# Swapping sample and prompt in the order of units of a hybrid trunk step

## The reference

```python
def trunk_layer(x, mod, p, ssd_h0, gdn_h0, kv_ctx):
    h = rmsnorm(x, p['norm1_w']) * (1.0 + sc1) + sh1
    u = h @ p['w_in']                       # 2584 columns, four head groups
    y = concatenate([ssd(u), gated_deltanet(u), fnet(u), attention(u)]) @ p['w_out']
    x = x + g1 * y                          # g1, sc1, sh1 ...: from silu(c) @ w_mod + b_mod
    h2 = rmsnorm(x, p['norm2_w']) * (1.0 + sc2) + sh2
    return x + g2 * peer(h2, p['peer_w_q'], p['peer_keys'], p['peer_u'], p['peer_v'])

def peer(x, w_q, sub_keys, u_tab, v_tab):   # 8 heads x 16 of 16384 experts a token
    idx, gate = ...                         # two-level top 16 of q @ keys
    act = gelu(einsum('ted,td->te', u_tab[idx], x))
    return einsum('te,ted->td', gate * act, v_tab[idx])
```

## Time and profile before

| | us |
|---|---|
| median of three runs | 3529.52 |
| lowest and highest | 3523.68, 3545.67 |
| the profiled execution | 3547.55 |
| its span in the profile | 3545.7 |

### The profile page before, as it was taken

How to read it: one execution, slowest core, us unless ns; L and a number is a source line. 1 busy time by engine, 2 the same in 40 slices (tenths; PEclk the granted TensorE clock), 3 DMA queues, 4 the chain that set the end, 5 groups by cost and what they waited for, 6 DMA issues and landing times.

```text
span 3545.7 us, 28928 instructions
## 1 busy us (share of the span) xinstructions
PE 2157.3 (61%) x10824; PEld 1423.2 (40%) x10824; DVE 1777.1 (50%) x3941; ACT 349.2 (10%) x765; POOL 1705.3 (48%) x1540
## 2 busy tenths in 40 slices
PE   7799446665893455537877766665885100027787
PEld 6689445553550355533525235553561000001111
DVE  0331477885119777791410457886107888850000
ACT  0211111111210000011111011111110000000000
POOL 0000045344334678874554556444334577776664
PEclk6775778786897555568998988786897555569999
DMA  5424268446685899998889888445676699999998
GB/s 158 154 72 137 81 237 325 143 161 218 222 300 213 316 395 394 395 381 298 310 324 334 316 292 324 166 161 195 225 273 216 218 367 369 371 372 369 346 367 314
DMA packets 380348, 960.02 MB, mean 271 GB/s; under 512 B 40857, under 2 KB 181529, under 8 KB 380081
## 3 DMA queue, kind: packets, MB, share of 16 engines
q0 software_dynamic: 221184, 805.40, 61.9%
q1 hardware_dynamic: 155456, 150.41, 12.9%
q10 hardware_dynamic: 3568, 2.36, 0.2%
HBM read 955.70 MB, written 2.36 MB: 270 GB/s over the span
## 4 chain that ended last, share of the span: by engine, by line
PE 22%; POOL 20%; DVE 17%; DMA 16%; issue 10%; ACT 2%; another core or an unknown queue 1%; POOLq 0%; SPq 0%; DVEq 0%; ACTq 0%
POOL sb_ring L550 20%; PE pb L571 15%; DMA sb_ring<-in_peer_v,sb_idxT 6%; PE pv L571 5%; DMA sb_wring<-in_w_in 4%; DVE sb_ring L1830 4%; DMA sb_wring<-in_peer_w_q 2%; DMA sb_ring<-in_peer_u,sb_idxu 2%; PE pb L574 1%; DVE sb_i16u L1759 1%; DMA sb_wring<-in_w_out 1%; DVE sb_pos L1759 1%; DVE sb_xe L1754 1%; ACT sb_hT L1050 1%; DVE sb_big L1536 1%
## 5 line engine op out<-in xcount | busy, mean ns | idle before, releaser
L550 POOL DMA_INDIRECT sb_ring<-in_peer_u,sb_idxu x768 | 963.4, 1254 | 1053.2 <-DVE sb_gatew L1802 461.7
L550 POOL DMA_INDIRECT sb_ring<-in_peer_v,sb_idxT x768 | 741.8, 966 | 766.3 <-PE pv L571 524.7
L1830 DVE CUSTOM_DVE_ANT_0 sb_ring<-sb_ring,sb_h 128x1024 f32<-128x1024 f32 x768 | 923.5, 1224 | 175.1 <-DMA sb_ring<-in_peer_u,sb_idxu 150.1
L571 PE MATMUL pv<-sb_ring,sb_wcol 128*32 128x512 f32 x3072 | 712.9, 652 | 163.1 <-DMA sb_ring<-in_peer_v,sb_idxT 136.5
L571 PE MATMUL pb<-sb_hT,sb_wring 128*128 128x256 f32 (+1 forms) x2304 | 439.7, 355 | 152.7 <-ACT sb_hT L1050 59.1
L571 PEld LDWEIGHTS pb<-sb_hT,sb_wring 128*128 128x128 f32 x2304 | 383.9, 212 | 226.6 <-ACT sb_hT L1050 61.5
L571 PEld LDWEIGHTS pv<-sb_ring,sb_wcol 128*32 128x32 f32 x3072 | 131.3, 115 | 687.1 <-DMA sb_ring<-in_peer_v,sb_idxT 454.9
L571 PE MATMUL pb<-sb_big 128*128 128x128 f32 (+2 forms) x1888 | 256.4, 307 | 64.9 <-DVE sb_big L1536 40.1
L571 PEld LDWEIGHTS pb<-sb_big 128*128 128x128 f32 (+1 forms) x1888 | 248.9, 217 | 81.7 <-DVE sb_big L1536 46.8
L571 PE MATMUL pb<-sb_cT,sb_wring 128*128 128x2 f32 x768 | 167.7, 353 | 144.8 <-DMA sb_wring<-in_w_mod 144.8
L574 PE MATMUL pb<-sb_cst,sb_dots 128*128 128x128 f32 x6 | 2.9, 475 | 391.1 <-DMA sb_ring<-in_peer_v,sb_idxT 364.3
(11 more groups left out here) (218 smaller groups left out, 1729.9 us busy)
## 6 DMA issues: line engine op xcount, KB each, us to landing
sb_wring<-in_w_mod SPq DMA_DIRECT2D x48, 1024.0 KB
sb_wring<-in_w_in SPq DMA_DIRECT2D x40, 1024.0 KB
sb_wring<-in_peer_w_q SPq DMA_DIRECT2D x32, 1024.0 KB
sb_wring<-in_w_out SPq DMA_DIRECT2D x16, 1024.0 KB
sb_ring<-in_peer_u,sb_idxu POOLq DMA_INDIRECT x768
sb_ring<-in_peer_v,sb_idxT POOLq DMA_INDIRECT x768
sb_cst<-in_cst SPq DMA_DIRECT2D x1, 1544.0 KB, 6.3
out<-sb_h ACTq DMA_DIRECT2D x3, 512.0 KB, 2.6
```

Of the source, the lines that this page charges most:

```text
L550: pool.indirect_dma_start(ring[:, j, :], None, a["tab_" + kind][l_of(q)], bass.IndirectOffsetOnAxis(ap=of, axis=0)).then_inc(rows_in[j], 16)
L571: return nc.tensor.matmul(out, lhsT, rhs, start=start, stop=stop)
L1830: dve.tensor_tensor_reduce(out=ring[:, j, :], in0=ring[:, j, :], in1=h2[:, t, :], scale=1.0, scalar=0.0, op0=ALU.mult, op1=ALU.add, accum_ ...
```

## The change

The list of units is turned within each layer: the sample comes first, then the prompt. With it the running numbers of tiles change, so that slots 0 to 3 begin at 0, 2, 3 and 5.

```diff
 GROUP_TILES = [[0], [1, 2]]
-UNITS = [(0, 0), (1, 0), (0, 1), (1, 1)]
+UNITS = [(1, 0), (0, 0), (1, 1), (0, 1)]
...
 def seq_tiles(u):
 
-    first = [0, 1, 3, 4][u]
+    first = [0, 2, 3, 5][u]
     return [(first + i, t) for i, t in enumerate(GROUP_TILES[UNITS[u][0]])]
```

## The result

| | before | after |
|---|---|---|
| median, us | 3532.5 (four runs) | 3692.1 (four runs) |
| lowest and highest | 3523.7, 3545.7 | 3681.9, 3708.0 |
| profiled execution (span) | 3547.55 (3545.7) | 3681.86 (3680.1) |

The ratio is 1.045, with a 95% interval of 1.040 to 1.050: the turned order is 4.5% slower, where 3725 us (5.5%) had been forecast. The same change timed on a second chip gave 1.050 [1.043, 1.058]. The two profiled executions lie at opposite ends of their ranges, so their spans differ by 134 us where the medians differ by 160.

The account below looks back on a forecast made before the run. The kernel was taken as paced by DMA where it is busy and by the mix's chain elsewhere. Slots 0 to 3 and tail: 244 + 170 + 7 + 145 - 370 = +196 us, on the median 3529.5 + 196 = 3725 us; range 3630 to 3850.

Parts of the forecast that it names:

- The blocks: Slot 0: the 16 blocks of w_mod sums woven into it cost 4.7 us each, 75 us in all.
- The sample's mix alone: Slot 0: 700 us of slot 3 less 66, 31 and 97, plus 31 us of block waits: 537 us.
- The dots half: Slots 1 and 3, up to the end of the intra stage: 256 rows with their dots and ten w_in blocks, 416 us.
- DVE becomes the bound: Slots 1 and 3, intra stage: dots and mix on DVE outlast the rows by 23 us, plus 12 in short stages.
- the tail's 177 us: Time of 128 rows in the tail, taken as the pace for 256 rows in slots 1 and 3: 354 us.
- The v half: Slots 1 and 3, after the dots: 188 + 186 us, twelve weight blocks, one handover and a hole, 446 us.
- The hole of 20 us: Slots 1 and 3, query stage: the next tile's v items must wait for its end; 80 matmuls without v, about 20 us.
- the handover: Slots 1 and 3: one change from dots to v matmuls, about 20 us.
- the one for fewer batches: Slot 2's mix: 17 of 64 batches lie in the sums, so 17/64 of 97 us of dots and v matmuls go, 26 us.
- Rival 1: Slots 1 and 3 run at 387 GB/s, 753 us each; kernel 3491 us on the median, 1.1% faster; chance 4%.
- Rival 2: Slots 1 and 3: the mix adds to the gathers, 950 us each, 160 us more together, 3885 us; chance 10%.
- rival 3: Slot 0's 16 blocks hide (-75 us) and layer 1's sums run at 2.4 GHz (-54): 3596 us, 1.9% slower; chance 12%.

Follow-up runs that it names:

- the freed `gelu`: The changed kernel with `gelu` and `end` also allowed at the points inside the query stage: 3604.7 us, 1.032 of the kernel before.

## Why the prediction was right, and where it wasn't

**The account by slot held.** Lost cover of the sample's mix, two slots of a fixed length under a prompt, one tile saved at the end; predicted and measured span by slot: 707 and 704, 870 and 846, 907 and 887, 870 and 851, 388 and 392. In sum 3742 and 3680 us, 62 us too much.

**Slot 0.** Right in sum through two errors of opposite sign. The blocks cost 58 us and not 75. The sample's mix alone had been put at 537 us, from slot 3's chain less the shares of dots, v matmuls and block waits; from its first normalisation (96 us) to the slot's end (704) it is 608 us, less 58, so 550. Taking shares of a chain away left 13 us too little. That the sum came within 3 us is luck.

**Slots 1 and 3.** The size was nearly right, the reason wrong. The dots half was forecast at 416 us and took 418. But it was built from 354 us of rows at the tail's pace, 27 us for bytes of the weight blocks, and 35 us in which "DVE becomes the bound". The bytes have no part in it (rows of half the length don't shorten it), and it isn't DVE that is late: POOL is. The step that failed is the reading of the tail's 177 us as the pace of transfers. The same row has POOL busy for 136.21 us with 129 gathers, and with 0.30 us between two of them that is 136 + 39 = 175 of the 177. POOL was the limit there, at 1.07 us a gather, and under denser dots a gather takes 1.34 (331.55 us for 248). 248 x (1.34 + 0.30) = 406 of the 418 us. So the match of 416 and 418 is luck. The sign stood in the trace of the kernel before, whose chain over the whole span has POOL's gathers first:

```profile
by line: POOL sb_ring L550 19.9%; PE pb L571 15.4%; issue 9.7%; DMA sb_ring<-in_peer_v,sb_idxT 6.4%; PE pv L571 4.9%; DMA sb_wring<-in_w_in 4.5%; DVE sb_ring L1830 4.1%; DMA sb_wring<-in_peer_w_q 2.1%; DMA sb_ring<-in_peer_u,sb_idxu 2.0%; P
```

The v half was forecast at 446 us, with 8 more for the unit's end, and took 428. The hole of 20 us was there (19 and 19 by the freed `gelu`). What was mis-sized are the terms beside the tail's 188 + 186 us and the hole: 32 us for the bytes of twelve weight blocks, 20 for the handover and 8 for the end, 60 us, which measured 428 - 374 - 19 = 35. The handover was counted twice, since the 188 us begin with one: POOL's one wait at it is 4.35 us in slot 1 and 3.76 us in the tail. And the rest isn't the bytes of the blocks: with gathers of half the bytes the DMA share is 0.63 there, and the half still takes 412 us, where two of that run's tail phases (180 us each) and the hole make 379. What the 35 us are stays open.

**Slot 2.** The sums took 252 us for 240, and their clock stayed at 0.50, that is 1.2 GHz, when gathers no longer interrupted them, with PE busy for 130.5 of 142 us. The rule of the Trainium skill that the prediction set aside (TensorE: Matmul & The Clock Gate, Part 1) would have had them speed up; the trace is against it for these matmuls of two columns. The mix after the sums took 635 us for 667. The step that was mis-sized is the one for fewer batches: 26 us had been taken off for dots and v matmuls alike, 17/64 of both. But a unit's u batches all go first, so the 17 that lie in the sums are dots alone, 17 of 32. On the chain of the 629 us from the first normalisation, dots are 2.8%, 18 us, where they were 66 (17/32 of these are 35), and v matmuls are 6.0%, 38 us, where they were 31. That makes 41 us off instead of 26. The other 17 of the 32 us no run assigns; block waits are one place, with w_in at 6.3%, 40 us, where it was 7.5%, 53 us.

**Rivals.** Rival 1 needed slots at DMA's pace; even with half of the bytes they stay at 844 us, so it was never near. Rival 2 (mix and gathers add up) didn't come, with 846 and 851 us where it had 950; what the dots delay is POOL. Of rival 3 one part is a small truth (blocks 17 us cheaper), the other false (the clock).

**What was not seen.** All signs named in advance appeared: first gather at 648 us, slots at 338 and 339 GB/s, DVE at 87% in the first half, no v matmul for 38 us in the query stage (1334 to 1372 us), sums that are quicker in their second half, a tail of 392. They would have appeared under either reason for the 850 us, so that they couldn't test it.

## What to carry to other kernels

Turning the order of two interleaved groups trades cover at the start for a shorter tail: here 241 us of bare mix and 272 us in two crowded slots went against 366 us of tail. Before a stretch is called bound by DMA because its share is 0.93, add up the engine that issues the transfers (406 of 418 us here), and test it with shorter rows, not with fewer partitions: a test that halves bytes counts only if the DMA share falls with them. Where an engine seems slow, compare the mean time of its one instruction between stretches; 1.34, 1.10 and 0.95 us for the same gather told what the busy shares didn't.

## What was new about the hardware

- A gather of 128 rows costs POOL 0.94 us and 0.30 us until the next, the same for rows of 4 and of 2 KB (966 and 979 ns on average in phase v). While DVE does dots of 1.22 us, it takes 1.10 us in the tail and 1.34 us in the dots half; with dots of 0.22 us it takes 0.95 us.
- Gathers to 64 partitions ran at 201 and 205 GB/s in the tail with a DMA share of 0.97 and 1.02, to 128 partitions at up to 404 GB/s with 1.02. The stretch that they shared with weight blocks took 390 us for 355.
- PE's granted clock stayed at 0.50 (1.2 GHz) through 142 us with PE 92% busy on matmuls of two columns.
